# A mixture-of-experts kernel: the next expert's first gate tile goes ahead of an expert's scatter, and the selection's transposes go behind the first up tile

## What is computed

```python
logits = t @ w_router + b_router
top_val, top_idx = lax.top_k(logits, TOP_K)          # TOP_K = 2 of 8
gates = jax.nn.softmax(top_val, axis=-1)
# for each expert e, over the tokens that chose it:
y = (silu(xb @ w_gate[e]) * (xb @ w_up[e])) @ w_down[e]   # 1024 -> 3584 -> 1024
out = out.at[tok].add(y * gate)
```

## Time and profile before

| what | value |
|---|---|
| runs | 1432.62, 1435.40 and 1435.53 us, median 1435.4 us |
| the profiled execution | 1433.9 us |
| its span in the trace | 1432.1 us |
| mean granted TensorE clock | 0.995 of full speed |
| PE busy, of the span | 98% |
| DVE busy | 79% |
| ACT busy | 65% |
| all traffic | 420 MB, 293 GB/s over the span |

### The profile page before, as it was taken

The page is one execution under the profiler, slowest core; times in us unless marked ns, Lnnn a source line. Parts: engine busy times, 40 slices in busy tenths (PEclk is TensorE's granted clock), DMA queues, the critical chain, the costliest instruction groups (busy, mean ns, idle before and its releaser), DMA issues.

```text
span 1432.1 us, 17664 instructions
## 1 busy us (share of the span) xinstructions
PE 1397.1 (98%) x6467; PEld 1144.5 (80%) x6467; DVE 1128.5 (79%) x808; ACT 934.4 (65%) x764; POOL 20.2 (1%) x28
## 2 busy tenths in 40 slices
PE   6999999999979999999999999999999999999997
PEld 5888888887868887888888788888878888887885
DVE  5454666655668888888888888888888888889887
ACT  5354434445657767777777777777777777777774
POOL 0000000000030000000000000000000000000000
PEclk9999999999999999999999999999999999999999
DMA  9358675453148998999999899999989999998992
GB/s 357 109 163 234 200 222 180 154 203 114 36 146 309 373 378 307 363 373 334 356 357 374 313 363 373 331 352 369 367 314 363 376 330 349 368 367 325 367 373 92
DMA packets 191689, 420.10 MB, mean 293 GB/s; under 512 B 19168, under 2 KB 21344, under 8 KB 191648
## 3 DMA queue, kind: packets, MB, share of 16 engines
q1 hardware_dynamic: 178432, 415.00, 80.7%
q10 hardware_dynamic: 12784, 3.26, 1.6%
q0 software_dynamic: 432, 1.28, 0.3%
HBM read 418.47 MB, written 1.05 MB: 293 GB/s over the span
## 4 chain that ended last, share of the span: by engine, by line
PE 92%; DVE 3%; ACT 2%; issue 2%; DMA 0%; POOL 0%; ACTq 0%; POOLq 0%; DVEq 0%
PE bank_G L1026 10%; PE bank_G L1028 10%; PE bank_G L1027 10%; PE bank_U L1026 9%; PE bank_U L1028 9%; PE bank_U L1027 9%; PE bank_Y L1026 8%; PE bank_Y L1028 8%; PE bank_Y L1027 8%; PE bank_T L1364 2%; DVE w_lo L646 1%; PE bank_G L1261 1%; PE bank_T L1026 1%; PE bank_T L1027 1%; PE bank_T L1028 1%
## 5 line engine op out<-in xcount | busy, mean ns | idle before, releaser
L646 DVE TENSOR_TENSOR w_lo<-raw,w_hi 128x2048 fp32r<-128x2048 f32 x391 | 890.3, 2290 | 210.2 <-ACT w_hi L381 209.6
L381 ACT ACTIVATE w_hi<-raw 128x2048 fp32r<-128x2048 f32 x391 | 749.2, 1918 | 294.1 <-PE bank_U L1028 95.8
L1026 PE MATMUL bank_Y<-w_hi,hidT_hi 128*128 128x512 f32 x492 | 194.1, 395 | 0.0
L1028 PE MATMUL bank_Y<-w_hi,hidT_lo 128*128 128x512 f32 x492 | 192.6, 391 | 0.0
L1027 PE MATMUL bank_Y<-w_lo,hidT_hi 128*128 128x512 f32 x492 | 192.1, 391 | 0.0
L1026 PE MATMUL bank_U<-w_hi,xg_hi 128*128 128x512 f32 x448 | 181.0, 404 | 0.4
L1026 PE MATMUL bank_G<-w_hi,xg_hi 128*128 128x512 f32 x448 | 176.9, 395 | 1.6 <-DVE w_lo L646 0.6
L1028 PE MATMUL bank_G<-w_hi,xg_lo 128*128 128x512 f32 x448 | 175.7, 392 | 0.0
L1028 PE MATMUL bank_U<-w_hi,xg_lo 128*128 128x512 f32 x448 | 175.6, 392 | 0.0
L1027 PE MATMUL bank_U<-w_lo,xg_hi 128*128 128x512 f32 x448 | 174.7, 390 | 0.0
L1027 PE MATMUL bank_G<-w_lo,xg_hi 128*128 128x512 f32 x448 | 174.7, 390 | 0.0
(11 more groups left out here) (262 smaller groups left out, 1467.3 us busy)
## 6 DMA issues: line engine op xcount, KB each, us to landing
raw<-in_expert_w_gate SPq DMA_DIRECT2D x112, 1024.0 KB, 7.1
raw<-in_expert_w_up SPq DMA_DIRECT2D x112, 1024.0 KB, 7.2
raw<-in_expert_w_down SPq DMA_DIRECT2D x112, 1024.0 KB, 7.0
raw<-in_nat_w_qkv SPq DMA_DIRECT2D x12, 1024.0 KB, 5.1
raw<-in_ffn_w_gate SPq DMA_DIRECT2D x11, 1024.0 KB, 8.1
raw<-in_ffn_w_up SPq DMA_DIRECT2D x11, 1024.0 KB, 5.1
raw<-in_ffn_w_down SPq DMA_DIRECT2D x11, 1024.0 KB, 5.2
raw<-in_fourier_w_in SPq DMA_DIRECT2D x4, 1024.0 KB, 11.4
```

What stands on the lines that cost most here:

```text
L381: nc.scalar.activation(w_hi[w][:], raw[s][:], ACT.Copy).then_inc(hi_made, 1)
L646: nc.vector.tensor_tensor(w_lo[w][:], raw[s][:], w_hi[w][:].bitcast(f32), ALU.subtract).then_inc(lo_made, 1)
L1026: nc.tensor.matmul(out_, xh, wh, start=start, stop=False)
L1028: return nc.tensor.matmul(out_, xl, wh, start=False, stop=stop)
```

## The change

PE runs an expert's scatter behind the next expert's gate tile 0, not ahead of it (`first_gate`, called before the loop and at the end of each pass). The selection's transposes, and PE's wait for the adds of the expert before, follow up tile 0. On DVE, `w_lo` of gate0b goes ahead of the two `y_lo`, `w_lo` of up0a and up0b go ahead of the four adds, and `next_selection` comes behind `hid` of step 0. ACT's order stays. Its loop, and those of DVE and SP, are cut one piece later (`AHEAD`), so that the piece gate0b belongs to the pass before.

```diff
+AHEAD = SPLIT + 1
...
         def own_loads(E):
-            for j in range(SPLIT, PER_EXPERT):
+            for j in range(AHEAD, PER_EXPERT):
...
         def next_loads(E):
-            for j in range(PER_EXPERT, PER_EXPERT + SPLIT):
+            for j in range(PER_EXPERT, PER_EXPERT + AHEAD):
...
         # ACT, expert(E, ahead)
             for j, (kind, c, half) in enumerate(EXPERT):
+                if j < AHEAD - SPLIT:
+                    continue
...
+            if ahead:
+                for j in range(PER_EXPERT + SPLIT, PER_EXPERT + AHEAD):
+                    split_hi(j, E)
...
         # DVE, expert(E, sweep, ahead)
             for j, (kind, c, half) in enumerate(EXPERT):
-                if (kind, c, half) == ("gate", 0, 1):
-                    next_selection(E, e, sweep, ahead)
-                elif (kind, half) == ("gate", 1):
+                if j < AHEAD - SPLIT:
+                    continue
+                if (kind, half) == ("gate", 1) and c:
                     hidden_rest(E, c - 1)
                 if (kind, half) == ("up", 1):
                     hidden(E, c)
+                    if c == 0:
+                        next_selection(E, e, sweep, ahead)
...
-                if (kind, c, half) == ("down", STEPS - 1, 0):
-                    continue
                 if (kind, c, half) == ("down", STEPS - 1, 1):
                     result_rest(E)
-                    if ahead:
-                        split_lo(j - 1 + SPLIT, E)
-                    add_result(E, e)
                 if ahead or j + SPLIT < PER_EXPERT:
                     split_lo(j + SPLIT, E)
+            if ahead:
+                for j in range(PER_EXPERT + SPLIT, PER_EXPERT + AHEAD):
+                    split_lo(j, E)
+            add_result(E, e)
...
         # PE
+        def first_gate(E):
+            pe.wait_ge(e_silu, E * STEPS)
+            columns(E, "gate", 0, G[0])
...
             for c in range(STEPS):
-                if c == 0:
-                    pe.wait_ge(e_silu, E * STEPS)
-                elif c == 1:
-                    pe.wait_ge(e_added, NB * E)
-                else:
-                    pe.wait_ge(e_silu, E * STEPS + (c - 1))
-                columns("gate", c, G[c % 2])
+                if c:
+                    if c >= 2:
+                        pe.wait_ge(e_silu, E * STEPS + (c - 1))
+                    columns(E, "gate", c, G[c % 2])
+                    hidden_transposes(c - 1)
+                if c != 1:
+                    pe.wait_ge(e_hid, E * STEPS + max(c - 1, 0))
+                columns(E, "up", c, U[c % 2])
                 if c == 0:
                     pe.wait_ge(e_added, NB * E)
                     pe.wait_ge(e_sel, E + 1)
                     for b in range(NB):
                         last = nc.tensor.transpose(T[1][:, P * b:P * (b + 1)], mo["sel"][:, b].bitcast(f32), ident[:])
                     last.then_inc(e_selT, 1)
-                else:
-                    hidden_transposes(c - 1)
-                if c != 1:
-                    pe.wait_ge(e_hid, E * STEPS + max(c - 1, 0))
-                columns("up", c, U[c % 2])
...
+            if ahead:
+                first_gate(E + 1)
             pe.wait_ge(e_selT_copy, E + 1)
-            if ahead:
-                pe.wait_ge(e_xlo, 2 * (E + 2))
             for q in range(2):
                 pe.wait_ge(e_ylo, 2 * E + 1 + q)
...
+        first_gate(0)
         with pe.Fori(0, LAST) as E:
             expert(E, True)
```

More of the change, by code:

```diff
@@ L310, in next_loads @@
         def next_loads(E):
-            for j in range(PER_EXPERT, PER_EXPERT + SPLIT):
+            for j in range(PER_EXPERT, PER_EXPERT + AHEAD):
                 src, tiles, _ = expert_source(ewg, ewu, ewd, (E + 1) % NE, j % PER_EXPERT)
                 load(j, E, src, tiles)
+        for j in range(SPLIT, AHEAD):
+            src, tiles, _ = expert_source(ewg, ewu, ewd, 0, j)
+            load(j, 0, src, tiles)
         with sp.Fori(0, LAST) as E:
@@ L616, in _ @@
         assert made[0] == N1
+        for j in range(SPLIT, AHEAD):
+            split_hi(j, 0)
         with act.Fori(0, LAST) as E:
@@ L989, in _ @@
         assert made[0] == N1
+        for j in range(SPLIT, AHEAD):
+            split_lo(j, 0)
         with dve.Fori(0, LAST) as E:
@@ L1342, in transpose_tokens, with columns @@
                 last.then_inc(e_xT, 1)
-        def expert(E, ahead):
[L1345 to L1355, removed]
+        def columns(E, kind, c, bk):
+            for half in range(2):
+                j = AT[kind, c, half]
+                ready(j, E)
+                if (kind, c) == ("gate", 0):
+                    pe.wait_ge(e_xlo, 2 * E + half + 1)
+                wh, wl = parts(j, E, KH)
+                for k in range(KH):
+                    kk = KH * half + k
+                    last = three(bk[:], mo["xg_hi"][:, kk], mo["xg_lo"][:, kk], wh[:, k], wl[:, k], kk == 0, kk == KD - 1)
+                last.then_inc(piece_used, 1)
+        def first_gate(E):
+            pe.wait_ge(e_silu, E * STEPS)
+            columns(E, "gate", 0, G[0])
+        def expert(E, ahead):
             def hidden_transposes(c):
@@ L1446, in _ @@
             transpose_tokens(NE + 1)
+            first_gate(NE)
             with pe.Fori(*SECOND) as E:
```

## The result

The changed kernel takes 1422.69 us (median of 4 runs, 1422.18 to 1424.05), against 1435.47 us for the kernel before in the same comparison (1432.62 to 1437.62): a ratio of 0.9913, 95% interval 0.9899 to 0.9927. I had forecast 1427.4 us, 8.0 less, and a range that ended at 1424.0. The direction was right, and the gain was larger than I had said: 12.8 us by the medians of the first comparison and 10.0 by those of the second.

What follows compares the result with a forecast made beforehand. PE, busy 98% of the span, was taken as the bound, with time to win only at its waits: 5.7 us at the scatter plus 2.3 at gate1a, 8.0 off 1435.4, gave 1427.4 us; range 1424.0 to 1432.0.

Steps and rivals of the forecast that it cites:

- The scatter: On PE at 7 expert borders, moving it behind gate tile 0 removes a 0.82 us wait each, 5.7 us.
- The wait at gate1a: PE's wait for `w_lo` at gate tile 1's first piece goes at experts 1 to 6, 2.3 us.
- Expert 0: Gains nothing at gate1a: no scatter stands between its gate and up tile 0; gate1a still starts at 439.18.
- The selection's transposes: On PE, moved behind up tile 0, they take 0.46 us wherever they stand.
- The scale: The 8.0 us gain was subtracted from the runs' median of 1435.4 us, not the profiled 1433.9.
- The range: Total time from 1424.0 to 1432.0 us; lower end from the runs' spread, upper end taking in the scatter-only case.
- Only the scatter's wait going: Rival: DVE runs 1.3 us late, so gate1a waits about as now; 1429.7 us, chance 0.11.
- both margins that I gave as 1.0 us: On PE at gate0b and gate1a, `w_lo` would be ready 1.0 us before it is needed.
- The adds blocking DVE: Rival: adds ahead of gate1a's `w_lo` hold up DVE's later pieces; slower, about 1439 us, chance 0.07.
- A late `y_lo`: Rival: `y_lo` behind gate0b's subtraction comes 2.6 us late, scatter waits as before; no change, 0.09 together with the transfers.
- The transfers: Rival: DMA becomes the bound, PE waits for data; no change, 1435.4 us, chance 0.09 together with a late `y_lo`.

Runs made afterwards that it cites:

- the second comparison: The changed kernel, unedited, run again with more runs against the kernel before: 1423.84 against 1433.84 us, ratio 0.9919.
- the experiment that takes this wait alone: Kernel before, with only `w_hi` of gate1a moved ahead of step 0's table load and silu on ACT: 1432.45 against 1434.18 us, ratio 0.9986.
- the last experiment: Changed kernel, with `w_hi` of gate1a moved ahead of silu of step 0 on ACT: 1423.4 us, ratio 0.9921 to the kernel before.
- three later edits: Changed kernel with `y_lo` ahead of gate0b's `w_lo`, 1432.1 us; adds ahead of up0b's `w_lo`, 1433.33; selection's transposes ahead of up tile 0, 1442.65.

## Why the prediction was wrong, point by point

*The scatter: right.* 0.82 us at 7 borders, 5.7 us, were forecast; moving the scatter was worth 0.85 us a border, 6.0 us, beyond what the other waits gave (periods of 124.23 and 123.38).

*The wait at gate1a: right.* 2.3 us in the changed kernel by my sum, and 3.0 with expert 0 for the experiment that takes this wait alone, which gave 3.2.

*Expert 0: right.* Its gate1a still waits for `w_lo`, 0.86 us behind the start of the transposes:

```profile
437.02 0.38 PE L1420 MATMUL bank_T<-ident,sel 128*128 128x128 f32 x2
437.88 0.51 PE L1041 MATMUL bank_G<-w_hi,xg_hi 128*128 128x512 f32 x1 [0.48 <-DVE w_lo L658]
```

*The selection's transposes: the step that failed.* "The selection's transposes, which take 0.46 us wherever they stand": they take 0.14. The other 0.32, and a slower restart of 0.03, were a wait for `w_lo` of up0a, which the reordering on DVE took away at experts 1 to 6 and in part at expert 7. That is 0.35 us at each of five experts and 0.26 at expert 1, 2.0 us, and it brings 8.0 to 10.0. Expert 7's border has 0.3 more: its pair took 0.33 us and now 0.14, and between the scatter and its gate tile 0 lay 0.35 us, now one pitch. Together they make 10.3 of the 10.4 measured. Three rows should have told me. In the same trace expert 0's pair took 0.14 us (432.84 to 432.98 above), and the four transposes of `hid` took 0.36. The subtraction that ended the wait could be placed from the earlier trace rows: the adds of 928.14 end at 930.8, and 2.35 later is 933.1. And expert 0, which has no adds in DVE's way, had its gate1a start 0.84 us behind the last matmul of up tile 0 where the others had about 0.5 and 0.3 more at the transposes: from gate0b's last matmul to gate1a it is 6.57 us in both cases (432.61 to 439.18, 932.42 to 938.99), the same chain of ACT and DVE. I had been looking for distances that were too long between matmuls and took the ones at transposes for granted.

*The scale: too high by 1.2 us.* I set the sum against the median of three runs, 1435.4 us; 29 later runs gave 1434.2. The 4.7 us between 1427.4 and the first result's 1422.69 are thus 2.4 of the sum, 1.2 of the scale and 1.1 by which those four runs lie under the later ones. With 10.4 us and the scale of 29 runs the time is 1423.8, and the second comparison measured 1423.84. That it agrees so closely is partly luck: from that comparison's own 1433.84 it would be 1423.4.

*The range* took its lower end from the spread of the runs alone. The price of a transpose pair had no bound from below in it. With 0.14 as the lower end (four transposes of `hid` cost 0.36), the range would have reached 2.2 us further down, to 1421.8, and held the time.

*The rivals.* Only the scatter's wait going: no, both margins that I gave as 1.0 us held (at gate0b 794.50 + 2.35 = 796.85 against 795.09 + 2.745 = 797.83, which is 0.98; at gate1a 804.94 + 2.35 = 807.29 against 808.06, 0.77, for PE is there earlier than I had it). The adds blocking DVE: not in this order, but shown to be real one place earlier. A late `y_lo`: no, both are done by 797.98, 2.6 us ahead of the scatter at 800.58. The transfers: no transfer ended a wait of ACT in any expert, at 356 GB/s over the period. The limit of about 358 GB/s in the Trainium skill's page "DMA: Bandwidth & Descriptors", section "Where 436 GB/s comes from", gives by estimate a period of at least 123.0 us for 42 pieces of 1 MB. 123.38 is above it, so the periods alone do not refute it; the stretch at 385 GB/s does, for ten microseconds at a time. The Trainium skill's page "ScalarE: Activation LUTs" gives about 1.38 us of draining beside each table load in "What ACT_TABLE_LOAD costs". These runs show nothing of it on either side of the load: in the last experiment the load starts at 434.70, 1.94 us behind the start of a `w_hi` of 1.92 us, and silu starts at 435.99, 1.29 us behind the load's start. With the Trainium skill's 1.38 us my estimate of the margin at gate1a was also too wide, 0.1 us where its own sum gives none (932.1 + 1.38 + 1.93 + 2.35 is 937.76, against 937.78).

## What to carry to other kernels

A distance between two instructions holds the price of the work and any wait that ends inside it; before a step is priced from such a distance, compare it with the same step where the suspected releaser is early, and add the hand-over to the start of every producer that PE needs next. Where engines hand pieces on in a fixed order, a new order can be laid out by hand from measured distances: here it gave five starts of DVE to 0.1 us, and foretold what three later edits would cost within 1.0 us (8.0, 9.5 and 19 against 9.0, 9.9 and 19.4 in the expert stretch). It is no better than its worst price: gate1a on PE was 0.3 us off by that of the transposes. And it has to be carried on behind the place that is edited: the last experiment missed because it was not. A baseline median from three runs was worth 1.2 us of error here, half as much as the term for gate1a.

## What was not expected of the hardware

A pair of 128-column transposes costs PE 0.14 us, and four cost 0.36 us, each with 0.08 us more for the slower start of the second matmul behind them. A wait can stand in the timeline with neither idle time nor a releaser: at 933.11 PE started 0.32 us later than two transposes require, but their record runs to 933.03. Only the comparison with expert 0, and the slightly longer first matmul (0.51 us in place of 0.48, with 0.34 to the second start in place of 0.31), give such a wait away. The start of the expert part lay up to 3.8 us apart in 12 profiles, and 1.9 us apart in two of the same kernel, while the 984 or 994 us behind it repeated to 0.1 us in each of the two kernels that were profiled twice. A table load was in one loop body twice a pass and in the other once, by whether the body began with a `w_hi` or a silu (764 and 757 instructions of ACT).
